# Combining six expert rows per token: sums on VectorE and one transpose, in place of three accumulating passes on TensorE

## What is computed

```python
def moe_ffn(h, ...):
    scores = sigmoid(h @ router_w)
    _, idx = top_k(scores + router_b, 6)
    w = take_along_axis(scores, idx); w = w / sum(w) * 2.5
    return routed_experts(h, idx, w, ...) + swiglu(h, s_gate, s_up, s_down)

# layer 0: 768 tokens (latent and context), layer 1: the 512 latent ones
xl = xl + g2 * out
# after layer 1
return rms_norm(xl, final_norm_w)
```

## Time and profile before

| | before |
|---|---|
| median of 3 runs | 3000.42 us |
| span of the profiled execution, its own time | 3001.2 us |
| PE busy | 2756.9 us (92%) |
| DVE busy | 906.9 us (30%) |
| ACT busy | 589.1 us (20%) |
| POOL busy | 422.4 us (14%) |
| L1536, the sums of the combine | 20 of 1.76 us |
| L832, the matmuls of the combine | 480 records, 63.6 us busy |

### The profile page before, as it was taken

How to read it: one execution, slowest core, us unless ns; L and a number is a source line. 1 busy time by engine, 2 the same in 40 slices (tenths; PEclk the granted TensorE clock), 3 DMA queues, 4 the chain that set the end, 5 groups by cost and what they waited for, 6 DMA issues and landing times.

```text
span 3001.2 us, 41007 instructions
## 1 busy us (share of the span) xinstructions
PE 2756.9 (92%) x16044; PEld 1999.4 (67%) x16044; DVE 906.9 (30%) x1560; ACT 589.1 (20%) x1124; POOL 422.4 (14%) x640
## 2 busy tenths in 40 slices
PE   6888899986999999999997898998699999999996
PEld 2454377544788788788786463764487887887885
DVE  2463655161111111111113576633211111111115
ACT  3312244030111111111111422422011111111111
POOL 0000000004222122122120000000421221221220
PEclk9998999997999999999998999999899999999998
DMA  7563000013778778888876320001488777777765
GB/s 293 215 249 135 1 1 1 28 43 131 295 304 321 302 302 330 315 308 312 325 300 231 114 74 14 1 15 56 177 314 308 289 298 296 300 297 294 295 264 199
DMA packets 97139, 626.39 MB, mean 209 GB/s; under 512 B 32048, under 2 KB 36912, under 8 KB 69936
## 3 DMA queue, kind: packets, MB, share of 16 engines
q1 hardware_dynamic: 53968, 562.34, 48.9%
q0 software_dynamic: 43104, 63.14, 5.7%
HBM read 628.99 MB, written 83.39 MB: 237 GB/s over the span
## 4 chain that ended last, share of the span: by engine, by line
PE 81%; DVE 8%; ACT 4%; DMA 4%; issue 2%; another core or an unknown queue 2%; SPq 0%; DVEq 0%; POOLq 0%; ACTq 0%
PE psum L801 33%; PE psum L816 17%; PE psum L498 15%; PE psum L681 3%; PE psum L657 3%; DVE arena L1498 2%; DMA arena<-in_mod_w 2%; ACT arena L1102 2%; PE psum L491 2%; PE psum L671 2%; PE psum L597 2%; DMA arena<-y 1%; DVE arena L1188 1%; PE psum L571 1%
## 5 line engine op out<-in xcount | busy, mean ns | idle before, releaser
L801 PEld LDWEIGHTS psum<-arena 128*128 128x128 f32 x8832 | 1010.4, 192 | 67.3 <-issue 67.3
L801 PE MATMUL psum<-arena 128*128 128x128 f32 x8832 | 1011.3, 275 | 1.7 <-DVE arena L1492 1.7
L498 PE MATMUL psum<-arena 128*128 128x512 f32 (+1 forms) x1360 | 525.6, 545 | 46.6 <-ACT arena L1090 15.8
L816 PE MATMUL psum<-arena 128*128 128x512 f32 x1104 | 506.7, 602 | 20.8 <-DVE arena L1498 11.1
L498 PEld LDWEIGHTS psum<-arena 128*128 128x128 f32 x1360 | 266.3, 199 | 299.3 <-issue 254.4
L816 PEld LDWEIGHTS psum<-arena 128*128 128x128 f32 x1104 | 198.4, 189 | 247.5 <-issue 247.5
L1498 DVE TENSOR_TENSOR arena<-psum,arena 128x256 f32<-128x256 f32 x138 | 58.5, 424 | 936.6 <-ACT arena L1102 936.6
L1587 POOL DMA_INDIRECT y<-arena,SIX x144 | 148.5, 1031 | 1166.1 <-DVE arena L1506 1126.4
L1506 DVE TENSOR_SCALAR arena<-psum,SIX 128x512 f32<-128x512 f32 x138 | 103.6, 751 | 440.1 <-PE psum L816 440.1
L1102 ACT ACTIVATE arena<-psum 128x256 f32<-128x256 f32 x138 | 52.9, 384 | 889.7 <-PE psum L801 889.7
L1110 ACT ACTIVATE arena<-psum,SIX 128x512 f32<-128x512 f32 x138 | 94.8, 687 | 451.5 <-PE psum L816 451.5
(11 more groups left out here) (194 smaller groups left out, 1708.6 us busy)
## 6 DMA issues: line engine op xcount, KB each, us to landing
arena<-in_experts SPq DMA_DIRECT2D x138, 3072.0 KB, 10.6
arena<-in_mod_w SPq DMA_DIRECT2D x48, 1024.0 KB, 7.3
arena<-y SPq DMA_DIRECT2D x20, 1536.0 KB, 16.8
arena<-in_wblk SPq DMA_DIRECT2D x22, 1024.0 KB, 4.8
arena<-in_shared SPq DMA_DIRECT2D x2, 3072.0 KB, 9.9
hrows<-arena SPq DMA_DIRECT2D x10, 512.0 KB
arena<-in_xT SPq DMA_DIRECT2D x1, 3072.0 KB, 16.4
y<-arena,SIX POOLq DMA_INDIRECT x144, 9.6
```

What stands on the lines that cost most here:

```text
L498: last = mm(job(l, key, n, parts), a, b, start=i == 0, stop=i == len(pairs) - 1)
L801: last = mm(psum[:, b, o * P:(o + 1) * P], WB[:, b, k * 512 + o * P:k * 512 + (o + 1) * P], HT[:, b, k, :], start=k == 0, stop=k == KC - 1)
L816: last = mm(psum[:, 3 + j, :], AT[:, b, f, :], WB[:, b, 4096 + f * D + j * 512:4096 + f * D + (j + 1) * 512], start=f == 0, stop=f == 1)
```

## The change

VectorE now adds all six rows. The first instruction is as before; two further adds of 512 values follow, row 1 onto row 0 and row 2 onto row 0, each ordered behind the one before by `link`, and `ysum` is raised by the last. TensorE transposes the one remaining row: 4 calls for each half where there were 12 matmuls.

```diff
@@ PE, the combine
                         for k in range(4):
                             m = 4 * i + k
-                            for y in range(3):
-                                last = mm(job(l, ("ct", t, i))[:, k * P:(k + 1) * P], Y6[:, t % 3, y, m * P:(m + 1) * P], ident,
-                                          start=y == 0, stop=y == 2)
+                            last = nc.tensor.transpose(job(l, ("ct", t, i))[:, k * P:(k + 1) * P],
+                                                       Y6[:, t % 3, 0, m * P:(m + 1) * P], ident)
                         last.then_inc(done, 1)
@@ DVE, the combine
                         y = Y6[:, t % 3, :, i * 512:(i + 1) * 512]
-                        V.tensor_tensor(y[:, 0:3, :], y[:, 0:3, :], y[:, 3:6, :], ALU.add).then_inc(sem(f"ysum{l}"), 1)
+                        link(V.tensor_tensor(y[:, 0:3, :], y[:, 0:3, :], y[:, 3:6, :], ALU.add))
+                        link(V.tensor_tensor(y[:, 0, :], y[:, 0, :], y[:, 1, :], ALU.add))
+                        V.tensor_tensor(y[:, 0, :], y[:, 0, :], y[:, 2, :], ALU.add).then_inc(sem(f"ysum{l}"), 1)
```

## The result

| | before | after |
|---|---|---|
| median of 5 runs (of before, two more than at the forecast) | 3001.57 us | 3013.87 us (3013.02 to 3015.52) |
| ratio | | 1.0039, 95% interval 1.0027 to 1.0052 |
| span of the profiled execution | 3001.2 us | 3013.3 us |
| combine of layer 0, first issue of rows to start of L491 | 58.13 us | 59.34 us |
| start of L491 to the first root of layer 1 | 7.15 us | 9.46 us |

The changed kernel is slower by 12.3 us in the median and 12.1 in the profiled executions. 12.13 of these lie in the three rows on the combines and L491 (1.21 + 2.31 + 8.61); everything else moved by less than 0.05 in all. The first issue of the rows was at 1611.58 and 2946.67 us before and is at 1611.12 and 2950.16 now.

What follows compares the result with a forecast made beforehand. Combines bound by expert-row landings in layer 0 and by DVE from tile 1 on in layer 1; 2.2 + 2.2 + 7.9 = +12.3 us gave a median of 3012.7 us, range 3007.5 to 3017.

Steps and rivals of the forecast that it cites:

- layer 0, DVE behind the landings: Layer 0 combine: most added time falls into landing waits, DVE never waits after 1639.47; +2.2 us, between 0 and 3.2.
- L491 starts at 1.2 GHz: L491 after layer 0's combine: PE, mostly idle, starts it at the lower clock; +2.2 us, bounds 0 and 2.6.
- layer 1, tile 0: First tile of layer 1's combine: fewer PE records let the next sum start earlier; -1.75 us, the only gain.
- layer 1, tiles 1 to 3: Layer 1 combine: two sums a tile in DVE's unbroken row, adds paid in full; +8.7 us.
- layer 1, last root: End of layer 1: L843's last 8 records run at 1.2 GHz before the root; +0.9 us.
- the pause in the landings: Layer 0 combine: DVE's 3.69 us of idle time before the sum at 1639.47, taken to stay.
- landings that move: Sign of being wrong: landings of layer 0 at other times than before the change.
- layer 0 hidden: Rival: the pause at 1639.47 moves or goes, landings cover nearly all of layer 0's adds; 3010.5 us, chance 0.12.
- clock kept: Rival: PE is at 2.4 GHz at L491 and L843, taking 3.1 us off; 3009.6 us, chance 0.13.
- Nothing hidden: Rival: in layer 0 all 12 pairs of adds count, 17.5 us in place of 2.2; 3028 us, chance 0.05.
- Not slower: Rival: PE's relief in layer 1's tile 0 outweighs the adds, if two cost below 0.46 us; about 3000 us, chance 0.06.

Runs made afterwards that it cites:

- the two changed kernels with fillers: Changed kernel plus 8 identity matmuls, or 8 one-column matmuls, ahead of each wait for a sum; first sum to L491 54.11 and 53.97 us.
- the run with one-column fillers: Changed kernel plus 8 matmuls of a single column ahead of each wait for a sum; layer 0 combine 60.36 us, L491 8.66 us.

## Why the prediction was right, and where not

| step | forecast | measured |
|---|---|---|
| layer 0, DVE behind the landings | +2.2 | +1.2 |
| L491 starts at 1.2 GHz | +2.2 | +2.3 |
| layer 1, tile 0 | -1.75 | -1.71 |
| layer 1, tiles 1 to 3 | +8.7 | +8.68 |
| layer 1, last root | +0.9 | +1.64 |
| all | +12.3 | +12.1 |

The forecast, 3012.7 us, stands against 3013.87 measured. The mechanism is the one foretold: two adds at the price of the nearest row, hidden where landings end last and paid in full where DVE does.

Two terms were mis-sized, and they nearly cancel: that the total fits to 0.2 us is luck. In layer 0 the sum was started from 1639.47, as if the pause in the landings stayed. It went, because the change itself took away the instructions whose fetch made it; DVE then became the bound two halves earlier, and the term is 40.6 us of work from 1629.77, +1.2 us on before. Of these 0.3 belong to a first landing that came later after its issue (6.44 us against 6.15), which the change does not explain; A' grew by 0.92. The prediction itself named landings that move as a sign of being wrong, and they did.

The working of the +2.2 was sound for its premise. In the two changed kernels with fillers, where the pause is back, A' is 2.1 and 2.2 us over before. The rival "layer 0 hidden" had the right case, with "other timing" for a cause, and a wrong sum: it let DVE be the bound from the third half on. A half without `gated` takes 3.12 us, so the fourth sum still waits for its landing (0.85 us). Counted from there, 1629.95 + 40.6 gives 1670.6 and a term of +0.9, which is what A' shows.

The last root cost 1.64 in place of 0.9: the prediction doubled only the last 8 records. At 1.2 GHz the 8 of the half before are still running when the last square is ready (at 3002.83), so all 16 lie on the path: 3.75 us where 2.12 had been.

The +2.2 for L491 was a choice between 0 and 2.6, and 2.3 came. In the other kernels whose L491 did not start at full clock it would have been 1.6 to 2.8, so the close fit of this term is in part luck as well.

The rival "clock kept" fell with B at 9.42 and the clock at 0.50 all through the combine. "Nothing hidden" fell with the kernel that changes layer 0 alone, 3.3 us and not 17.5. "Not slower" fell at its own condition: an add costs 0.69 us, and the relief in tile 0 is the only gain.

## What to carry to other kernels

Moving work from the busiest engine of the whole to an idle one pays only where the busiest one ends last; in this combine it was DMA in one layer and VectorE in the other, and each was to be read from the stage. Price an added operation from the nearest row of the same size and count it for each unbroken stretch of its engine; where it lies in front of a landing wait, compute how much of the wait is left. TensorE, when it is relieved, may fall to its lower clock and charge that to its next real work. A few dummy matmuls in a wait known to be long can buy it back (ratio 0.9980 here), but the run that had them in the combine of layer 1 as well lost 1.6 us there, in part by a landing that a moved instruction fetch made late. So where instructions are added or removed, look which transfers the instruction fetches then fall among.

## What the runs showed of the hardware

- Transposes alone brought PE from 0.50 to full clock (24 in 2.84 us, PEclk 1.00). In the same run, after 2.35 us without work, the clock was once still 1.00 (at 1638.4) and once 0.51 (at 1648.1).
- PE can be busy and slow: in the run with one-column fillers it was busy 16.49 of 17.00 us and its clock stayed at 0.50:

```profile
1628.00:1645.00 17.00, 16.49 (x80) 16.34 (x79) 15.28 (x27) 0.00 (x0) 0.00 (x0) 0.50 1.05 387
```

- One packet of instruction fetch holds up one of the sixteen parts of a stream of large transfers by 1.2 to 1.5 us (landings 5.45 us apart in place of 4.06), while the rate of all queues stays at 387 GB/s. The lost time shows only at the landings, and a second packet later in the same stream cost nothing.
